# A hybrid block on one core: ScalarE's table loads asked for ahead of three square roots and, in sixteen heads, by one table set for logarithm and exponential

## The reference, cut to what matters

```python
y = (xf - mu) * lax.rsqrt(var + LN_EPS) * g + b           # norms: a Sqrt on ScalarE, a reciprocal on VectorE

log_f = jnp.logaddexp(jnp.log(lb), jnp.log1p(-lb) + jax.nn.log_sigmoid(a))
key = (1.0 - lb) * jax.nn.sigmoid(-a)                     # heads: Sigmoid and Ln
decay = jnp.exp(jnp.where(lower_tri, diff, -jnp.inf))     # Exp
scores = jnp.einsum("bhtk,bhsk,bhtsk->bhts", qb, kb, decay)
o = rms_norm(o_fwd + o_bwd, o_norm)                       # per head, by Ln and Exp(-0.5 x)
```

## Time and profile before

| | |
|---|---|
| runs (three) | 2662.75, 2664.54, 2668.41 us |
| median | 2664.54 us |
| span of the profiled execution | 2672.6 us |
| time of the profiled execution beyond its span | not recorded |
| instructions | 42756 |
| mean granted TensorE clock | 0.979 |
| TensorE busy | 95% |
| VectorE busy | 75% |
| ScalarE busy | 52% |
| GpSimd busy | 31% |
| stage of the heads | about 2014 to 2592 us of the span |

### The profile page before, as it was taken

How to read it: one execution, slowest core, us unless ns; L and a number is a source line. 1 busy time by engine, 2 the same in 40 slices (tenths; PEclk the granted TensorE clock), 3 DMA queues, 4 the chain that set the end, 5 groups by cost and what they waited for, 6 DMA issues and landing times.

```text
span 2672.6 us, 42756 instructions
## 1 busy us (share of the span) xinstructions
PE 2551.9 (95%) x16588; PEld 2319.3 (87%) x16588; DVE 1997.6 (75%) x2574; ACT 1395.7 (52%) x2181; POOL 819.6 (31%) x765
## 2 busy tenths in 40 slices
PE   6799999999999999999999989999899999999979
PEld 3678888889977888888888879999789999999978
DVE  7889878878878785555554679898668888888855
ACT  0344334444455454445544477676556666676652
POOL 0100001002245420001111338984105555666630
PEclk8799999999999999999999989999899999999989
DMA  9988766887866885555555534444445444444434
GB/s 348 353 285 272 250 221 206 272 278 256 291 207 208 273 272 202 190 178 190 189 188 185 190 100 158 154 147 158 141 159 181 142 149 147 156 151 150 153 102 148
DMA packets 147009, 534.60 MB, mean 200 GB/s; under 512 B 16855, under 2 KB 17016, under 8 KB 146424
## 3 DMA queue, kind: packets, MB, share of 16 engines
q1 hardware_dynamic: 143480, 519.82, 58.1%
q0 software_dynamic: 3328, 12.06, 1.4%
HBM read 525.52 MB, written 6.29 MB: 199 GB/s over the span
## 4 chain that ended last, share of the span: by engine, by line
PE 71%; DVE 13%; issue 7%; ACT 6%; DMA 2%; POOL 1%; SPq 0%; ACTq 0%; DVEq 0%; POOLq 0%
PE ps L595 34%; PE ps L599 22%; PE ps L597 5%; PE ps L598 5%; DVE wl L1045 4%; ACT wh L1775 2%; DVE ps L1524 2%; DVE misc L1066 1%; DMA AF<-in_w_ada 1%; PE ps L982 1%; PE ps L728 1%; PE ps L740 1%; DVE BF L1674 1%; PE ps L657 1%; DVE BF L1664 1%
## 5 line engine op out<-in xcount | busy, mean ns | idle before, releaser
L1045 DVE TENSOR_TENSOR wl<-ring,wh 128x1024 fp32r<-128x1024 f32 x784 | 1040.8, 1339 | 392.2 <-ACT wh L1775 351.9
L599 PE MATMUL ps<-A,wl 128*128 128x256 f32 x4480 | 1265.9, 283 | 0.0
L1775 ACT CAST wh<-ring 128x1024 fp32r<-128x1024 f32 x784 | 814.6, 1044 | 356.2 <-PE ps L599 340.2
L599 PEld LDWEIGHTS ps<-A,wl 128*128 128x128 f32 x4480 | 858.0, 192 | 0.4
L595 PE MATMUL ps<-A,wh 128*128 128x512 f32 x2176 | 780.3, 403 | 24.3 <-DVE wl L1045 9.5
L597 PE MATMUL ps<-A,wh 128*128 128x256 f32 x2304 | 674.7, 293 | 15.3 <-DVE A L1049 9.8
L595 PE MATMUL ps<-B,wh 128*128 128x512 f32 x1792 | 641.4, 402 | 20.7 <-DVE wl L1045 8.7
L598 PE MATMUL ps<-A,wh 128*128 128x256 f32 x2304 | 653.9, 284 | 0.0
L595 PEld LDWEIGHTS ps<-A,wh 128*128 128x128 f32 x2176 | 412.5, 190 | 126.8 <-DVE wl L1045 10.9
L599 PE MATMUL ps<-B,wl 128*128 128x256 f32 x1792 | 504.4, 281 | 0.0
L597 PEld LDWEIGHTS ps<-A,wh 128*128 128x128 f32 x2304 | 443.7, 193 | 18.9 <-issue 10.0
(11 more groups left out here) (251 smaller groups left out, 2174.1 us busy)
## 6 DMA issues: line engine op xcount, KB each, us to landing
ring<-in_w_m SPq DMA_DIRECT2D x256, 512.0 KB, 4.6
ring<-in_hgrn_w_in SPq DMA_DIRECT2D x160, 512.0 KB, 3.8
ring<-in_w_ada SPq DMA_DIRECT2D x146, 512.0 KB, 5.2
ring<-in_w_in SPq DMA_DIRECT2D x144, 512.0 KB, 5.6
ring<-in_conv_w_in SPq DMA_DIRECT2D x96, 512.0 KB, 3.9
AF<-in_w_ada SPq DMA_DIRECT2D x46, 512.0 KB, 8.5
ring<-in_w_ab SPq DMA_DIRECT2D x32, 512.0 KB, 5.6
ring<-in_w_o SPq DMA_DIRECT2D x32, 512.0 KB, 5.6
```

What stands on the lines that cost most here:

```text
L599: return e.matmul(dst[:, 0:256], lo, x[:, 0, :], start=False, stop=last)
L1045: e.tensor_tensor(low[:], ring[SLOT[h]][:], hi[:].bitcast(F32), ALU.subtract).then_inc(s.lo, 1)
L1775: e.copy(wh[h % NSPLIT][:], ring[SLOT[h]][:]).then_inc(s.hi, 1)
```

## The change

Four requests for tables are added to ScalarE's program, and nothing else. Three ask for the set that holds Sqrt: in the last turn of the loop over `w_o`, ahead of that turn's waits; at tick LAST_TILE + 12 of the convolution, ahead of the waits for the mean; and behind the loop over the convolution's output projection, ahead of the last operand's square. The fourth asks in each head, behind the waits of step 0 and ahead of its Ln, for the set that holds both Ln and Exp. [...]

```diff
             squares_early(n, 0)
+            if n == 15:
+                e.preload_act_table(ACT.Sqrt)
             w.wait_ge(s.mm, H_WO + 2 * n + 2)
...
             if tick == LAST_TILE + 12:
+                e.preload_act_table(ACT.Sqrt)
                 w.wait_ge(s.mean, 4 + 16)
                 w.wait_ge(s.cpad, 16)
                 e.activation(left_sq[:], mean_ap, ACT.Square).then_inc(s.dd, 1)
...
+        e.preload_act_table(ACT.Sqrt)
         next_operand(15)
         next_high(15)
...
                 w.wait_ge((s.kq0, s.kq1)[u], 17 * t - 3)
                 w.wait_ge((s.cum0, s.cum1)[u], 2 * t)
+            e.preload_act_table_set("natural_log_exp_and_others")
             for k in range(2):
                 e.activation(slot(u, 6 + k), sig[0][:, 256 * k:256 * k + 256], ACT.Ln,
```

## The result

The changed kernel takes 2652.06 us in the median of 4 runs (2649.32 to 2655.05), the kernel before 2666.47 us beside it on the same chip (4 runs). The ratio is 0.9944, 95% interval 0.9933 to 0.9955: 14.9 us faster, between 12.0 and 17.9. The profiled execution took 2649.32 us with a span of 2647.4, so 1.9 us lie outside the span. A second round of six runs gave 2648.56 against 2663.82 us, ratio 0.9942 (0.9929 to 0.9955).

A forecast was written before the change was run, and what follows sets the result against it. ScalarE's burst of loads at each head's start was taken to set the 35.28 us period, making TensorE wait at the transposes; 9.5 + 1.3 + 2.3 + 0 - 0.4 = 12.7 us less, 2664.5 to 2651.8 us, range 2646 to 2659.

The forecast's parts named there:

- The mechanism: Heads: one load fewer per steady burst brings ScalarE's path to 34.00 us, below TensorE's 34.48; TensorE then sets the pace.
- Rival A: Transposes at L965: waits stay from a second cause just as late; only 3.2 us gained, 2661.3 us; chance 0.09.
- Rival C: Heads: the request does not count for the later Ln, one load more per burst; 17.9 us, total 2682.8; chance 0.05.
- Heads: Transposes at L965: each of 12 heads gives back only TensorE's wait, 0.79 us; 9.5 us together, 0.49 becomes slack.
- Rival B: Heads: TensorE's share is smaller than recorded, 12 heads each give a whole load; 18.6 us, 2645.9 us; chance 0.04.
- Last projection: Behind the last projection: the last burst's saved load frees the bank TensorE waits 6.54 us for; 1.3 us gained.
- Last two heads: Heads 14 and 15: Ln and Exp loads fall away; 0.7 + 0.3 + 1.3 = 2.3 us gained.
- First norm: First norm: the load fits ScalarE's idle time but was mostly hidden before; 0, between -0.1 and +0.1 us.
- The convolution's norm: Request directly behind a weight cast delays the square and VectorE's variance; costs 0.4 us, ends 0 and 1.28.
- A gain is excluded: Convolution's norm: no gain possible from the request, since no path to the square root gets shorter.
- Norm before the heads: Load is free in ScalarE's 3.02 us idle; inverse deviation 1.28 us earlier, but no TensorE wait follows before the heads: 0.
- The drain of the Trainium skill: Table switches: the skill adds a 1.38 us drain to the load, some 14 us gain in all; the trace speaks against it.

The follow-up runs named there:

- the second profile: The changed kernel run again without an edit, against the kernel before: 2648.56 us (six runs) against 2663.82, ratio 0.9942.

## Why the prediction was right, point by point

The forecast of 2651.8 us stands against 2652.06, and 12.7 us of gain against 14.9 (12.0 to 17.9) and, in the second round, 15.5 (12.0 to 18.9). The closeness of the sum to the median is partly luck: the terms for the heads, the last projection and the last heads were too small, and in the first profile they come to 17.4 where the runs give 14.9.

- **The mechanism** held: 31 loads, the transposes' waits gone, TensorE as the next bound. Rival A fell with the missing wait. Rival C fell with the loads. Its price per head was right: three loads in the burst gave a period of 36.54, 1.26 above 35.28. Its sum was too small, for the first two heads are slowed by 2.7 and 2.0 us and not by one load between them: from the first transposes to the restart behind the last projection it is 540.5 us for 519.5, 21.0 more, where C had 17.9. The 2687.28 us, 19.8 above the 2667.52 beside it, lie near C's 18.3 only because the last two heads of that kernel lack the loads that C would have.
- **Heads, 9.5 predicted, 11.8 measured.** The step that was off is "each head gives back only its wait, 0.79". The period fell by 0.98, so 12 x 0.98 = 11.8. TensorE's own pace is 34.30, not 35.28 - 0.80 = 34.48, and the slack about 0.3, not 0.49. The wait as recorded was smaller than what it cost, and the rows show where the rest lies. In the stream the matmuls start 0.12 us apart though each is recorded with 0.28. After the change the transposes start 2131.99 - 2131.86 = 0.13 us behind the last L599, before the change 2140.96 - 2139.88 = 1.08 behind it. That is 0.95 to 0.96 later, while the recorded wait counts only from that matmul's recorded end, 0.16 into it. The remaining 0.03 is in the transposes themselves, 0.41 for 0.38. Rival B had the direction and the reason right, with 0.18 per head in place of 0.48.
- **Last projection, 1.3 predicted, 2.0 measured** (6.54 to 4.53). Besides the load of the last burst, the backlog that VectorE carried from one burst to the next came back. Before, the eviction L1725 followed its predecessor with no gap; after, VectorE is idle for 0.49 us ahead of it, and ScalarE's Sigmoid waits for it 1.29 us for 0.68. In the last burst, counted from the last transposes ahead of the restart, L1725 starts 7.49 us behind them for 8.26, and VectorE's split 14.95 for 16.98: 0.77 from the backlog and the load on top. The prediction had treated the last burst as if it began at the same place against TensorE's work. For the same reason VectorE's gap ahead of its split is 2.57 us where 2.2 was forecast, and the wait behind the last projection 4.53 where 5.3 was. Together 13.8; TensorE's time from its first transposes in the heads to the restart behind the last projection fell from 519.5 to 505.4 us, 14.1.
- **Last two heads, 2.3 predicted, 3.5 or 2.6 measured.** The loads were priced right. Head 14: the three waits ahead of L991 and of the two groups of L982 before it came to 0.89 + 0.88 + 0.96 = 2.73 us and come to 1.06 + 0.15 + 0.80 = 2.01, which is 0.7 for 0.7. Head 15: from the end of the row sums L657 to the restart it was 4.77 us and is 3.23, which is 1.5 for 0.3 + 1.3. Together 2.2. What was put at nothing is TensorE's clock: L991 and L657 together took 3.26 us and take 1.83, or 2.85 in the second profile, that is 1.4 or 0.4 more. The rest, at most 0.2 us the other way, lies ahead of L991. The last wait itself is 2.89 or 2.59 us, for 1.8 to 2.8 forecast. I did not name the clock, for the waits of the earlier trace rows made me look at waits only. The runs with loads put back agree: head 15 alone costs 33.64 - 32.08 = 1.6 us against the changed kernel's second profile, whose L991 is nearly as slow, and head 14 1.07, of which 0.36 is L991 (2.04 for 1.68). The kernel with one load more per head has L991 at 2.04 too and takes 31.90 us, 2.8 less than before; 0.5 of that is no load either, for there the clock rose 4.2 us behind the restart and not 5.5.
- **First norm:** 0.13 gained, just beyond my +0.1: the reciprocal now follows the centring 1.13 us behind its start, for 1.24.
- **The convolution's norm, 0.4 lost predicted, 0.8 or 0 measured.** The order of events was right; the size was not. I let the square end 1.28 later than it had. But before, the square began 0.1 us before the recorded end of the cast (1860.37 for 1860.46), and now it begins 0.01 behind the end of the load; and VectorE, which had found its operand ready, now waits for it (0.54 us); the centring then follows 0.51 behind the variance, for 0.34. This makes 0.63 at the variance and 0.80 at the reciprocal. It then reaches TensorE (42.92 for 42.15) unless the meeting of VectorE and GpSimd goes VectorE's way; in the profiles where it did, the loss was gone. "A gain is excluded" holds for the request; that it could be masked was not foreseen.
- **Norm before the heads:** nothing, as predicted; the kernel with the norms' requests alone is at 1.0007.
- **The drain of the Trainium skill** ("ScalarE: Activation LUTs", section "What ACT_TABLE_LOAD costs"), with which a switch would be about 2.66 us: in the burst with two loads in a row they start 1.29 us apart and the Ln 1.30 after the second. No drain shows, and three loads cost 1.26 more than two.

The sum with the measured terms is 11.8 + 2.0 + 3.5 + 0.1 - 0 = 17.4 in the first profile and 11.8 + 2.0 + 2.6 + 0.1 - 0.8 = 15.7 in the second; the runs say 14.9 and 15.5. The 17.4 belong to one execution that kept its clock and had no loss at the convolution, and lie within the interval's end at 17.9.

**The best version** is likely the change without the convolution's request. It was 2.2 us under the changed kernel on the same chip, and their six runs each do not overlap (2643.44 to 2647.64, 2647.77 to 2650.52). In the two profiles 0.8 us of this is the convolution's norm and 0.8 the clock at the end, which was kept in one and lost in the other; the rest lies in stretches that neither kernel changes. The kernel with the heads' request alone, which lacks the convolution's too, has a ratio of 0.9940 in another round, so the intervals of all these versions overlap. That this version is better is not shown.

## What to carry to other kernels

A table load counts where ScalarE's burst sets the period of the loop, and only as far as the next engine's own pace: count the loads in the burst, and measure the period with one more and one less. Ask for a set ahead where ScalarE is idle anyway. Behind back-to-back work a request only moves the load in front of something that others wait for. And a request lasts until another head's function or request replaces the set.

## What was not expected of the hardware

- A wait recorded with 0.80 us cost 0.98 us of the period. TensorE's matmuls are recorded with 0.28 us each and start 0.12 us apart, so the recorded wait leaves out the 0.16 us by which a next matmul would have run into the record of the last one.
- With the same instructions and the same recorded waits ahead (1.06, 0.15, 0.80 us), TensorE kept the granted clock of 1.00 through L991 in one profile of the kernel (1.13 us) and lost it in another (1.63 us, mean of 0.59 over the 2 us from 2561.00). It goes with how soon behind the last projection's restart the clock had risen; what decides that stays open. At the last restart the clock is 0.50 in the first profile and 1.00 in the second, where TensorE had stood for 2.59 us (first matmul 0.80 us and 0.50).
- Where VectorE and GpSimd meet at the same two operations, either may be the one held up, by 0.5 to 0.7 us an operation (VectorE 0.95 for 0.41, GpSimd 1.53 for 0.87). The starts are 0.19 us apart in both cases, so these rows do not show what decides it.
